# The state-space stage of a two-layer encoder: another order on the sync queue, a scratch laid out by row, gated products between the last outputs

## The reference, cut to what matters

```python
def s5_mixer(h, w_in, lam_re, lam_im, log_dt, b_re, b_im, c_re, c_im, d_skip, w_glu):
    u = (h @ w_in).reshape(B, S, G, C)              # 64 groups of 16 channels
    ...                                             # discretised A, B from lam, dt
    bu = einsum('bsgc,gpc->bsgp', u, bbar)          # complex, 64 states a group
    x = associative_scan(combine, (a, bu), axis=1)  # x[s] = a * x[s-1] + bu[s]
    y = einsum('bsgp,gcp->bsgc', xr, c_re) - einsum('bsgp,gcp->bsgc', xi, c_im)
    y = gelu(y.reshape(B, S, W) + d_skip * u.reshape(B, S, W))
    val, gate = split(y @ w_glu, 2)
    return val * sigmoid(gate)
```

## Time and profile before

| | |
|---|---|
| median of 3 runs | 1189.56 us |
| runs | 1190.89, 1185.75, 1189.56 us |
| span of the profiled execution | 1193.3 us (first to last instruction; a time of the whole execution is not given for it) |
| PE busy | 1131.6 us (95%) |
| DVE busy | 814.4 us (68%) |
| ACT busy | 456.3 us (38%) |
| mean granted clock of PE | 0.977 |

### The profile page before, as it was taken

The page is one execution under the profiler, slowest core; times in us unless marked ns, Lnnn a source line. Parts: engine busy times, 40 slices in busy tenths (PEclk is TensorE's granted clock), DMA queues, the critical chain, the costliest instruction groups (busy, mean ns, idle before and its releaser), DMA issues.

```text
span 1193.3 us, 14622 instructions
## 1 busy us (share of the span) xinstructions
PE 1131.6 (95%) x5596; PEld 918.5 (77%) x5596; DVE 814.4 (68%) x1151; ACT 456.3 (38%) x677; POOL 128.0 (11%) x222
## 2 busy tenths in 40 slices
PE   6998999999989999899999979998999999999995
PEld 4776558788877888688777877887888888888874
DVE  6886655798888787777666873554775377635664
ACT  5422553454523544225452313333443234423431
POOL 3837107900000000000000000000000000000000
PEclk9999999999989999899999979999999999999997
DMA  6232002233334423333254873332323333233221
GB/s 215 74 94 89 1 1 71 71 105 107 107 114 144 131 89 109 120 125 106 95 170 135 246 203 88 110 98 76 103 93 99 95 97 98 88 106 92 93 80 70
DMA packets 61749, 125.60 MB, mean 105 GB/s; under 512 B 21744, under 2 KB 30320, under 8 KB 61680
## 3 DMA queue, kind: packets, MB, share of 16 engines
q1 hardware_dynamic: 60528, 120.48, 32.3%
q0 software_dynamic: 1152, 4.19, 1.1%
HBM read 109.97 MB, written 14.68 MB: 104 GB/s over the span
## 4 chain that ended last, share of the span: by engine, by line
PE 82%; DVE 9%; issue 4%; ACT 2%; DMA 1%; DVEq 1%; SPq 0%; ACTq 0%
PE bank L1166 25%; PE bank L1168 25%; PE bank L1167 25%; DVE WL L657 1%; PE bank L1381 1%; DVE MX L775 1%; PE bank L1373 1%; DVE SS L668 1%; PE bank L1332 1%; DVE Pexp L783 1%; ACT WH L424 1%; DMA TM<-kd_scratch 1%; PE bank L1184 1%; PE bank L1179 1%; DMA RAW<-in_w_win 0%
## 5 line engine op out<-in xcount | busy, mean ns | idle before, releaser
L424 ACT ACTIVATE WH<-RAW 128x1024 fp32r<-128x1024 f32 (+1 forms) x184 | 190.2, 1034 | 470.5 <-PE bank L1168 436.1
L1166 PE MATMUL bank<-GH,WH 128*128 128x512 f32 x816 | 323.9, 397 | 16.8 <-DVE GL L695 11.9
L1168 PE MATMUL bank<-GH,WL 128*128 128x512 f32 x816 | 320.0, 392 | 0.0
L1167 PE MATMUL bank<-GL,WH 128*128 128x512 f32 x816 | 319.9, 392 | 0.0
L657 DVE TENSOR_TENSOR WL<-RAW,WH 128x1024 fp32r<-128x1024 f32 (+1 forms) x184 | 223.1, 1212 | 45.5 <-ACT WH L424 45.0
L1166 PE MATMUL bank<-AH,WH 128*128 128x512 f32 x596 | 236.6, 397 | 3.7 <-DVE AL L895 2.6
L1167 PE MATMUL bank<-AL,WH 128*128 128x512 f32 x596 | 233.5, 392 | 0.0
L1168 PE MATMUL bank<-AH,WL 128*128 128x512 f32 x596 | 233.4, 392 | 0.0
L1166 PEld LDWEIGHTS bank<-GH,WH 128*128 128x128 f32 x816 | 154.6, 189 | 52.8 <-issue 17.7
L1167 PEld LDWEIGHTS bank<-GL,WH 128*128 128x128 f32 x816 | 154.6, 189 | 32.8 <-issue 1.2
L1168 PEld LDWEIGHTS bank<-GH,WL 128*128 128x128 f32 x816 | 154.4, 189 | 32.6
(11 more groups left out here) (228 smaller groups left out, 1000.7 us busy)
## 6 DMA issues: line engine op xcount, KB each, us to landing
RAW<-in_w_up SPq DMA_DIRECT2D x88, 512.0 KB, 3.5
RAW<-in_w_dn SPq DMA_DIRECT2D x32, 512.0 KB, 3.4
RAW<-in_w_glu SPq DMA_DIRECT2D x16, 512.0 KB, 3.6
RAW<-in_w_dn SPq DMA_DIRECT2D x16, 384.0 KB, 3.0
RAW<-in_w_wo SPq DMA_DIRECT2D x8, 512.0 KB, 3.5
od_scratch<-OO SPq DMA_DIRECT2D x8, 512.0 KB, 3.1
kd_scratch<-KT SPq DMA_DIRECT2D x8, 512.0 KB, 5.2
O<-od_scratch POOLq DMA_DIRECT2D x8, 512.0 KB, 4.5
```

What stands on the lines that cost most here:

```text
L424: act_(WH[b % RH][:, :n], RAW[b % RW][:, :n], ACT.Copy).then_inc(s_hi, 1)
L1166: mm(out, wh, hi_[:, k, :], start=start, stop=False)
L1167: mm(out, wh, lo_[:, k, :], start=False, stop=False)
L1168: return mm(out, wl, hi_[:, k, :], start=False, stop=stop)
```

## The change

- The sync queue's round t: u_out(t) goes ahead of load(win+4+t); lags_in(t-1) moves from behind y_out(t-3) to behind the load, ahead of u_in(t); u_in(t), y_out(t-3) and y_in(t-3) follow.
- `lags_in(j)` from j = 2 on waits on a new semaphore TM_used, which PE increments after the TM half of each outputs; until now it followed a transfer that waited for gelu.
- `kd_scratch` has TM's layout: KT is stored by 8 transfers for each tile, one a group (16 partitions, pieces of 512 B with a stride of 4 KB), and TM is read as rows of 4 KB. The waits on `kd_written` count 8 times as much.
- DVE's y_lo moves one round later (t - 5 for t - 4, with one more round).
- On PE, slices 0 and 1 of glu blocks 0 and 1 stand between outputs(6) and outputs(7) (before: slices 0 to 3), and slices 2 to 5 behind it (before: 4 and 5).

```diff
--- before.py
+++ after.py
@@ -274,7 +274,7 @@
         bank = [ctx.enter_context(nc.psum_tensor(f"bank{i}", [P, S], F32)) for i in range(8)]
 
         OD = nc.dram_tensor("od_scratch", (NJ, P, 2, QJ * C * LQ), F32, kind="Internal").ap()
-        KD_ = nc.dram_tensor("kd_scratch", (NJ, P, LQ, C * LQ), F32, kind="Internal").ap()
+        KD_ = nc.dram_tensor("kd_scratch", (NJ, P, GJ, C * LQ), F32, kind="Internal").ap()
         UD = nc.dram_tensor("ud_scratch", (NJ, P, LQ, NK), F32, kind="Internal").ap()
         YD = nc.dram_tensor("yd_scratch", (NJ, P, LQ, NK), F32, kind="Internal").ap()
 
@@ -297,6 +297,7 @@
         s_tmr, s_or = [sem("TM0"), sem("TM1")], [sem("O0"), sem("O1")]
         s_uw, s_ur = sem("ud_written"), [sem(f"U{i}_loaded") for i in range(3)]
         s_rt, s_E, s_X, s_Y, s_g = sem("RT"), sem("E"), sem("states"), sem("Y"), sem("gelu")
+        s_tm = sem("TM_used")
         s_yw, s_yr = sem("yd_written"), [sem("YB0_loaded"), sem("YB1_loaded")]
         s_sig = sem("sigmoid")
         s_fin, s_out = sem("final"), sem("out_written")
@@ -352,7 +353,9 @@
 
             def lags(j):
                 sp.wait_ge(s_kt, j + 1)
-                sp.dma_start(KD_[j], KT[:]).then_inc(s_kw, 16)
+                for g in range(GJ):
+                    sp.dma_start(KD_[j].rearrange("(c t) g m -> c t g m", t=LQ)[:, :, g],
+                                 KT[C * g:C * g + C]).then_inc(s_kw, 16)
 
             for b in range(4, FIRST["win"] + 4):
                 load(b)
@@ -384,24 +387,25 @@
                 sp.dma_start(YB[j % 2][:], YD[j]).then_inc(s_yr[j % 2], 16)
 
             def lags_in(j):
-                k = KD_[j]
-                sp.dma_start(TM[j % 2][:], bass.AP(k.tensor, k.offset, [[C * LQ, P], [C * LQ * P, GJ], [1, C * LQ]])
-                             ).then_inc(s_tmr[j % 2], 16)
-
-            sp.wait_ge(s_kw, 16 * NJ)
+                if j >= 2:
+                    sp.wait_ge(s_tm, j - 1)
+                sp.dma_start(TM[j % 2][:], KD_[j]).then_inc(s_tmr[j % 2], 16)
+
+            sp.wait_ge(s_kw, 16 * GJ * NJ)
             sp.wait_ge(s_wcs, 1)
             sp.wait_ge(s_act, TILE0["h02"] + THIRDS[2][1])
             lags_in(0)
             lags_in(1)
             for t in range(NJ + 3):
                 if t < NJ:
+                    u_out(t)
                     load(FIRST["win"] + 4 + t)
-                    u_out(t)
+                if 3 <= t < NJ + 1:
+                    lags_in(t - 1)
+                if t < NJ:
                     u_in(t)
                 if t >= 3:
                     y_out(t - 3)
-                    if t - 1 < NJ:
-                        lags_in(t - 1)
                     y_in(t - 3)
             for b in range(FIRST["win"] + 4 + NJ, NBLOCKS):
                 load(b)
@@ -540,7 +544,7 @@
                 act.wait_ge(s_etc, j + 1)
                 act.wait_ge(s_k0, j + 2)
                 if j >= 1:
-                    act.wait_ge(s_kw, 16 * j)
+                    act.wait_ge(s_kw, 16 * GJ * j)
                 strip = KP[:]
                 lags = bass.AP(strip.tensor, LQ - 1, [[C * (2 * LQ - 1), P], [-1, LQ], [2 * LQ - 1, C], [1, LQ]])
                 act_(KT[:].rearrange("p t (c s) -> p t c s", s=LQ), lags, ACT.Copy).then_inc(s_kt, 1)
@@ -986,13 +990,13 @@
                 v.tensor_tensor(AL[:, j, :].rearrange(t, s=LQ), YB[j % 2][:],
                                 AH[:, j, :].bitcast(F32).rearrange(t, s=LQ), ALU.subtract).then_inc(s_act, 1)
 
-            for t in range(NJ + 4):
+            for t in range(NJ + 5):
                 if t < NJ:
                     u_out(t)
                 if 2 <= t < NJ + 2:
                     states(t - 2)
-                if t >= 4:
-                    y_lo(t - 4)
+                if t >= 5:
+                    y_lo(t - 5)
 
             for i in range(KD):
                 b = FIRST["glu"] + 2 * i
@@ -1370,8 +1374,9 @@
                     pe.wait_ge(s_g, j - 1)
                 for gi in range(2):
                     for q in range(QJ):
-                        mm(bank[4 + 2 * p + gi][:, q * NK:(q + 1) * NK], TM[p][:, 2 * q + gi, :], U2[j % 3][:, 2 * q + gi, :],
-                           start=(q == 0), stop=False, skip_group_check=True)
+                        m = mm(bank[4 + 2 * p + gi][:, q * NK:(q + 1) * NK], TM[p][:, 2 * q + gi, :],
+                               U2[j % 3][:, 2 * q + gi, :], start=(q == 0), stop=False, skip_group_check=True)
+                m.then_inc(s_tm, 1)
                 pe.wait_ge(s_X, j + 1)
                 pe.wait_ge(s_or[p], 16 * (j // 2 + 1))
                 for r, x in enumerate((XR, XI)):
@@ -1405,9 +1410,9 @@
             outputs(NJ - 3)
             inputs(NJ - 1)
             outputs(NJ - 2)
-            glu_part((0, 1), range(0, 4))
+            glu_part((0, 1), range(0, 2))
             outputs(NJ - 1)
-            glu_part((0, 1), (4, 5))
+            glu_part((0, 1), range(2, 6))
             glu_part((2,), range(0, 6))
             glu_part((0, 1, 2), (6,))
             glu_part((0, 1, 2), (7,))
```

## The result

The changed kernel took 1195.0 us (median of 20 executions, 1187.33 to 1199.21), the kernel before 1190.8 us (20 executions, 1185.7 to 1195.81). The ratio is 1.0032, 95% interval 1.0016 to 1.0048: some 3.8 us longer. That is inside the 0.5% bound of "same", but it has the other sign than my 1183.0 and lies above the range's 1188.5. The profiled execution has a span of 1197.1 us (its own time 1198.87) against 1193.3 before, at a mean clock of 0.974. In the measurements behind this one, single executions of 1288, 1912 and 2922 us lie far outside all others and are left out of the ratios.

A forecast was written before the change was run, and what follows sets the result against it. TensorE (PE), busy 95% of the span, was taken as the bound. Terms -9.9 (end), +0.45 (opening) and +2.8 (clock) gave -6.6 us off the 1189.56 median: 1183.0, range 1178.5 to 1188.5.

The forecast's parts named there:

- U(7) then lands near 699, since a load and TM(6) are ahead of it.: End of the stage, sync queue: the last read of U arrives near 699, before PE wants it at 700.2.
- the new order stores UB(7) at 691.1, as soon as it exists: Round 7, sync queue: UB(7)'s store starts at 691.1, where it started at 693.69 behind a weight load.
- The steady rounds have nothing to give: Rounds from 652 to 696: no long pause stands in PE's waits, so no time can be gained there.
- the third case: Queue still late at the stage's end: U(7) near 703, clock falls as before, -2 us, some 1187.5; chance 0.17.
- forecast of -9.9: End of the stage on PE: 9.9 us gained, from 6.2 idle less a 1.75 pause, and some 5.4 of clock.
- the opening, +0.45 us: Start of the stage: load(win+5) arrives 0.45 us later, so PE's 0.8 us pause for states(0) grows to 1.2.
- the wait for TM(6) goes: Before outputs(6): TM(6) lands by 698 to 700.3, before PE wants it at 701.3, removing a 3.85 us wait.
- the pause of 1.75 us and the clock in it: Before outputs(6)'s state half: PE waits 1.75 us for XI(6), and one fall of the clock there costs 2.8 us.
- the second case: End of the stage: the clock stays up in the 1.75 us pause, giving 1180.1 us; chance 0.20.
- y_lo is not late: End of the stage: y of tile 7 is ready near 724.4, PE wants it at 725.4; costed at nothing.
- kd_scratch costs nothing: Stores of KT: eight issues take 3.4 us a tile, within a cover of 8.7 us, so no cost.
- the fourth case: Eight kd_scratch writes a tile hold up weight loads: slower, some 1203 at 1.3 us an issue; chance 0.05.

The follow-up runs named there:

- e4: Changed kernel with y_in(t-4) behind u_out(t), in place of y_in(t-3) at the end of the round before; 1188.35 us, ratio 0.9959.
- e6: Changed kernel with lags_in(t-1) back behind y_out(t-3), UB's store still ahead of the weight load; 1188.07 us, ratio 0.9962.
- e9: Changed kernel with load(win+4) first, u_in ahead of y, y_in a round later, lags_in last in most rounds, glu block 3's load behind round 7; 1187.39 us.
- e10: As e9, plus states(6) ahead of y_lo(2) on DVE and three gated slices, not two, ahead of outputs(7); 1186.26 us, ratio 0.9953.
- e8: Kernel before with only the later y_lo and the moved gated products; ratio 1.0012.
- e5: Changed kernel with rounds 0 to 2 in the old order, then u_out, y_in(t-4), u_in ahead of weight load, lags_in, y_out; 1190.27 us, ratio 0.9986.
- before_again: The kernel before, unchanged, profiled a second time; span 1192.9 us.
- before_again2: The kernel before, unchanged, profiled a third time; span 1185.0 us.

## Why the prediction was wrong

- **Failed: "U(7) then lands near 699, since a load and TM(6) are ahead of it."** That step gave the read 4.5 us behind two large transfers. It measured 7.2 (7.18 in the change, 7.2 in e4, where the queue is not late), close to the estimate of 3.3 us plus what the transfers ahead take of the engines; 6.6, 6.7 and 4.6 us in the other profiles of the change. I had no row of a small read behind two large ones. In the kernel before, the load ahead of u_in has landed by the time its store has, and TM stands behind it. By itself this costs the 2.00 us of e4, and a fall of the clock.
- **Failed: "the new order stores UB(7) at 691.1, as soon as it exists".** It was stored at 697.11: 2.6 us later because UB(7) itself came later, after the opening, and 3.4 us late on the queue. I replayed the last round alone. The same queueing makes y's stores of the rounds land after 6.6 to 8.0 us, for which the forecast had no price (its 3.6 is for the last tile), and y_in waits for them at the end of every round. So the queue's last turns took 11.8 and 11.9 us against PE's 10.6, and the lateness of the kernel before, whose last turns took 11.2 and 11.9, did not go. e6 and e4, which break this loop in different ways, both remove the lateness and run 0.4% below the kernel before. The sentence "the steady rounds have nothing to give" was right, and hid that they had something to lose.
- The two steps and the opening add up: U(7) landed at 707.7 where the forecast had 699, 2.6 us by the later UB(7), 3.4 by the late store and 2.7 by the longer read. The store's landing, 3.36 us for 3.4, was right.
- Together these are the third case, "the queue is still late", to which I gave 0.17. Its mechanism was right, its price was not: I had U(7) near 703 and -2 us; it came at 707.7, and the end, 38.1 us for 38.5, gave nothing back. Of the forecast of -9.9 the profile shows -0.4. The forecast's argument against this case, that the store starts 2.6 us earlier, is what did not come true.
- **Mis-sized: the opening, +0.45 us.** In the profile, opening and rounds took 2.6 us more, and 1.8 on the average of three profiles of each kernel. I looked only at the load that is late for ACT, and not at what the load does to the read behind it: the wait for U(0) is 0.69 us. The pause for XI was 0.93, 0.1 more than before and under the forecast 1.2. The remaining 1.7 us is the clock, which fell near 653 and which I had left out here though the pause lies among the same 64-column products. It fell there in two of the four profiles of the change; in the other two, after pauses of 1.05 and 0.25 us, it did not, nor in the three of the kernel before.
- **Right: the wait for TM(6) goes.** No profile of the changed kernel has it; lags_in's wait on TM_used held the queue once, for 0.4 us.
- **Right, but not seen in the changed kernel itself: the pause of 1.75 us and the clock in it.** e9 shows both, with the end 31.3 us for the 31.4 of the replay. The Trainium skill, TensorE: Matmul & The Clock Gate, section "HAM oscillation — how this bites in real kernels", warns of longer pauses only; e9 (1.75 us) and e10 (0.76 us) both saw the clock at 0.50 behind the pause, so the row of the kernel before was the right guide, and the second case's rule did not hold.
- **Right: y_lo is not late, and kd_scratch costs nothing**, though one term was mis-sized. KT's stores in the changed kernel, their group, one tile's run with the next load, and ACT's copy of that load's block:

```profile
L357 SPq DMA_DIRECT2D kd_scratch<-KT x64: 561/599/1818, 323.0 to 550.4; - x64
```

```profile
400.15 5.06 SPq L357 DMA_DIRECT2D kd_scratch<-KT  x8
405.25 0.59 SPq L328 DMA_DIRECT2D RAW<-in_w_up  x1
```

```profile
412.39 1.06 ACT L428 ACTIVATE WH<-RAW 128x1024 fp32r<-128x1024 f32 x1 [2.35 <-PE bank L1172]
```

Eight issues took 5.1 us, not 3.4, and the next load went out 1.45 us later than in the earlier trace rows. ACT's copy stands where it stood, released by PE and not by the load: hidden. They land in a median of 2.6 us each and overlap. The Trainium skill, DMA: Bandwidth & Descriptors, section "Rules for kernel authors", calls transfers under 64 KB mostly overhead; at 64 KB none of that reached PE, and the 16 us of the fourth case did not come. The fixed 2 us that the prediction takes from the same page of the Trainium skill stand there for transfers issued by GpSimd (section "Anatomy of one DMA — SWDGE (gpsimd) path"); these are issued by SP.

What stays open. The stretch is 1.6 us longer over the profiles and the timed ratio says 3.8; seven profiles, in which the stretch of each kernel spreads over 3 us, can't tell whether the rest is in the chance of a fall of the clock. e8's stretch in one profile is 2.3 us shorter than the mean of the kernel before, and its ratio of 1.0012 does not confirm it. Why the kernel before waited 0.32 us for TM(6) in one profile and 3.1 to 3.9 in the others was not found. That GpSimd's fetch of O is part of U's 7.2 us is argued from its place in time; no run moved it. The bytes ahead on the queue are not all of it: in e6 only the load stands ahead of U(7), TM behind it, and the read still took 6.3 us. Which share is whose stays open.

## What to carry to other kernels

A small transfer on this queue cost its own landing plus the time of the large ones issued ahead of it (3.3 us became 6.4): price it by the bytes in front and by what runs beside it, not by its landings in the old order. When an order is changed, add up one whole turn of the queue, with the landings that it waits for, and hold it against the bottleneck engine's round, in the old order as well. Where it is longer, the lateness grows each round and the last one pays: 0.6, 1.0, 2.1 and 3.4 us in the changed kernel. Moving the large transfer back is only free if its own consumer, and what stands behind that on its engine, has the slack (e5). What helped was to wait for a store's landing only behind the next round's first store (e4, e9).

## What the runs showed of the hardware that I had not expected

- The clock: among products of 64 columns a pause as short as 0.76 us was followed by a fall (e10 at 704, with one of 0.83 some 6 us earlier), and one of 0.77 us by a fall in one kernel (e9 near 652, a clock of 0.58 over 652 to 656) and by none in another (e10, 1.00). The same pause of 0.76 us at 650 was followed by a fall in e5 (0.57 over 652 to 656) and by none in the kernel before (1.00), which have the same order on the sync queue in rounds 0 to 2. The size of the pause alone does not decide.
- The span of one unchanged kernel is 1192.9 or 1185.0 us, at a mean clock of 0.977 and 0.984. Windows of the two profiles, before_again and before_again2, columns as in the earlier trace rows, show part of it long before the stage:

```profile
30.00:60.00 30.00, 27.78 (x122) 22.46 (x121) 23.79 (x32) 13.75 (x20) 26.02 (x25) 0.94 0.25 79
```

```profile
30.00:60.00 30.00, 26.86 (x124) 21.57 (x123) 23.28 (x32) 14.29 (x21) 26.06 (x24) 1.00 0.27 84
```

- Issuing a store in pieces of 512 B took the sync queue 0.56 to 1.82 us, median 0.60, against 0.33 to 0.97, median 0.43, for the old stores of KT. An issue right behind the transfers of U or y took longer still: a weight load 2.03 us at 637.41 in the change, and TM, in 4 KB rows, 3.84 us at 655.07 in e10. So the new layout did not end such long issues of TM; its place had more to do with them. In the change, ahead of u_in, TM's issues took at most 0.49 us, and in e6, with the same layout behind y_out, up to 3.09.
